# A mixer whose planner, output projection, softmax sums and score products are changed

## The reference

```python
def sandwich(x, y_fn, g_pre, g_post, shift, scale, gate, weight):
    h = rms_norm(x, g_pre) * (1.0 + scale[:, None, :]) + shift[:, None, :]
    y = rms_norm(y_fn(h), g_post)
    return x + weight * gate[:, None, :] * y

# the mixer, one input projection into six parts
qa, ka, va, qb, kb, vb = split(h @ w_in + b_in)
# A: 8 query heads of 64, 2 key heads; own chunk of 64 tokens + 2 before; ALiBi bias, a sink per head
# B: 8 heads of 64; own chunk + 8 before; clipped relative-position bias
p = softmax(q @ k.T / 8 + bias)          # A: exp(sink) is added to the sum
y = concat([rms_norm(oa, g_grp_a), rms_norm(ob, g_grp_b)]) @ w_out + b_out

swiglu = (silu(h @ w_gate) * (h @ w_up)) @ w_down     # inner width 2816
```

## Time and profile before

| | us |
|---|---|
| median of three runs | 1387.67 (1387.14 to 1389.07) |
| profiled execution, its own time | 1383.58 |
| span of its slowest core, which the page shows | 1382.0 |
| spans of the eight cores | 1373.8 to 1382.0 |
| mixer of the first half, L695 to the last chunk | about 301 to 558 |
| mixer of the second half | about 949 to 1215 |

### The profile page before, as it was taken

The page is one execution under the profiler, slowest core; times in us unless marked ns, Lnnn a source line. Parts: engine busy times, 40 slices in busy tenths (PEclk is TensorE's granted clock), DMA queues, the critical chain, the costliest instruction groups (busy, mean ns, idle before and its releaser), DMA issues.

```text
span 1382.0 us, 21264 instructions; the slowest of 8 cores (1373.8 to 1382.0 us)
## 1 busy us (share of the span) xinstructions
PE 1290.0 (93%) x7661; PEld 630.5 (46%) x7661; DVE 468.7 (34%) x866; ACT 442.1 (32%) x870; POOL 191.5 (14%) x382
## 2 busy tenths in 40 slices
PE   2799999999889999999999999999988899999997
PEld 1344444554444544444444444444544454444443
DVE  2131112442543455212442111243245344521122
ACT  2241112333545542111432111233455645311110
POOL 3011001130111112001230001112011011200000
PEclk9999999999999999999999999999999999999999
DMA  9998978657134428994558656202512242899111
GB/s 179 182 191 149 171 126 130 113 86 133 17 69 103 82 51 147 171 154 135 156 151 166 118 110 105 49 1 58 96 32 36 57 70 54 155 166 169 44 47 61
DMA packets 32094, 148.21 MB, mean 107 GB/s; under 512 B 3274, under 2 KB 8567, under 8 KB 20344
## 3 DMA queue, kind: packets, MB, share of 16 engines
q0 software_dynamic: 26128, 129.64, 53.4%
q1 hardware_dynamic: 5864, 17.22, 3.5%
HBM read 258.36 MB, written 8.40 MB: 193 GB/s over the span
## 4 chain that ended last, share of the span: by engine, by line
PE 84%; DMA 5%; DVE 4%; issue 3%; ACT 2%; POOL 1%; DVEq 0%; ACTq 0%; POOLq 0%; another core or an unknown queue 0%
PE psall L660 21%; PE psall L619 17%; PE psall L622 16%; PE psall L774 9%; PE psall L695 6%; PE psall L984 4%; DMA RING<-w_gu 3%; PE psall L882 2%; PE psall L877 1%; PE psall L912 1%; PE psall L650 1%; PE psall L709 1%; DMA R<-w_ada 1%; PE psall L525 1%; DMA RING<-w_in 1%
## 5 line engine op out<-in xcount | busy, mean ns | idle before, releaser
L660 PE MATMUL psall<-R 128*128 128x512 bf16 x1320 | 288.6, 379 | 0.0
L619 PE MATMUL psall<-HT,RING 128*128 128x512 bf16 x928 | 220.9, 381 | 5.4 <-DMA RING<-w_gu 5.3
L629 DVE TENSOR_TENSOR R<-SG,psall 128x512 bf16<-128x512 f32 x136 | 93.5, 688 | 379.2 <-ACT SG L627 353.1
L622 PE MATMUL psall<-HT,RING 128*128 128x512 bf16 x928 | 219.4, 379 | 0.0
L627 ACT ACTIVATE SG<-psall 128x512 f32<-128x512 f32 x136 | 81.2, 597 | 375.1 <-PE psall L622 375.0
L660 PEld LDWEIGHTS psall<-R 128*128 128x128 bf16 x1320 | 128.3, 98 | 151.2
L774 PE MATMUL psall<-HT,RING 128*128 128x512 bf16 x640 | 147.3, 382 | 3.5 <-ACT HT L510 1.7
L619 PEld LDWEIGHTS psall<-HT,RING 128*128 128x128 bf16 x928 | 90.6, 98 | 114.6 <-issue 7.6
L622 PEld LDWEIGHTS psall<-HT,RING 128*128 128x128 bf16 x928 | 90.9, 98 | 109.9 <-issue 0.8
L569 DVE TENSOR_TENSOR XH<-psall,GG 128x1024 f32<-128x1024 f32 x48 | 58.7, 1223 | 205.2 <-ACT SG L561 183.5
L561 ACT ACTIVATE SG<-psall 128x1024 bf16<-128x1024 f32 x48 | 49.1, 1023 | 237.3 <-PE psall L660 188.5
(11 more groups left out here) (136 smaller groups left out, 1109.0 us busy)
## 6 DMA issues: line engine op xcount, KB each, us to landing
RING<-w_gu POOLq DMA_DIRECT2D x53, 1024.0 KB, 10.3
R<-w_down POOLq DMA_DIRECT2D x44, 512.0 KB, 16.9
R<-w_ada POOLq DMA_DIRECT2D x10, 1024.0 KB, 20.3
RING<-w_in POOLq DMA_DIRECT2D x10, 1024.0 KB, 9.7
RING<-w_ada POOLq DMA_DIRECT2D x8, 1024.0 KB, 9.6
out<-X SPq DMA_DIRECT2D x16, 512.0 KB, 2.6
R<-w_gu POOLq DMA_DIRECT2D x5, 1024.0 KB, 53.1
X<-x POOLq DMA_DIRECT2D x8, 512.0 KB, 26.4
```

The source lines that it names most:

```text
L619: e.matmul(PS[bG][:], lhsT=rb[:, k, jj * 128:(jj + 1) * 128], rhs=HT[:, k, tb * 512:(tb + 1) * 512], start=(k == 0), stop=(k == 7))
L622: ins = e.matmul(PS[bU][:], lhsT=rb[:, k, 256 + jj * 128:256 + (jj + 1) * 128], rhs=HT[:, k, tb * 512:(tb + 1) * 512], start=(k == 0), sto ...
L629: S.op('dve', (lambda e, bU=bU, sgi=sgi, j=j, tb=tb: e.tensor_tensor(out=AT[:, tb, j, :], in0=SG[:, sgi, :], in1=PS[bU][:], op=ALU.mult)), ...
L660: ins = e.matmul(PS[bk][:], lhsT=AT[:, t // 4, j, (t % 4) * 128:(t % 4 + 1) * 128], rhs=WD[:, j, hh * 512:(hh + 1) * 512], start=(j == 0), ...
```

## The change

Outside the mixer only names and the model's numbers change. In the mixer:

- **Model.** `LAT` is a number for each engine instead of 0.2 for all; several costs are others, above all that of a value unit.
- **Score products.** `pads`, `QAP` and `QBP` go. `s_pair` does both heads of each partition block together: two table products into two banks, and then products of 64 rows, the lower and the upper half of the partitions in turn, each half into its own bank. For B the heads are put into the order 0, 2, 4, 6, 1, 3, 5, 7.
- **Weight tiles.** Ten `PT` tiles; the four new ones lie where the padded queries were. The mask has a tile of its own.
- **Softmax sums.** For each of the three banks in turn: add the sink's exponential (zero for B), reciprocal, product.
- **Output projection.** The two banks are two steps, each with its own hold, square and gate.

```diff
-EST = {'pe': 0.2, 'act': 0.62, 'dve': 0.68, 'pool': 0.6, 'sp': 0.1}
-LAT = 0.2
+EST = {'pe': 0.2, 'act': 0.55, 'dve': 0.68, 'pool': 0.6, 'sp': 0.1}
+LAT = {'pe': 0.28, 'act': 0.15, 'dve': 0.15, 'pool': 0.15, 'sp': 0.1, 'dma': 0.1}
...
-HORDER = [0, 1, 2, 3, 4, 5, 6, 7]
+HORDER = [0, 2, 4, 6, 1, 3, 5, 7]
...
-    NPT = 6
+    NPT = 10
...
+    def half_square(bank, c):
+        S.op('act', lambda e: e.activation(out=JNK[:, 0:512], in_=PS[bank][:], func=AF.Square, scale=1.0 / 32,
+                                           accum_out=ST[:, c:c + 1]),
+             reads=[ps_key(bank)], writes=[("sg", 0), ("st", c)], cost=0.82)
+
+    def half_gate(t, hh, bank, c):
+        cs = slice(hh * 512, (hh + 1) * 512)
+        S.op('dve', lambda e: e.tensor_tensor(out=XH[:, t % 2, cs], in0=PS[bank][:], in1=GG[:, cs], op=ALU.mult),
+             reads=[ps_key(bank), ("gg",), ("st", c)], writes=[("xh", t % 2)], cost=0.68)
+
+    def half_root(c):
+        S.op('pool', lambda e: e.tensor_tensor(out=ST[:, c:c + 1], in0=ST[:, c:c + 1], in1=ST[:, c + 1:c + 2], op=ALU.add),
+             reads=[("st", c), ("st", c + 1)], writes=[("st", c)], cost=0.35)
...
+            sb_ = [SBANKS[(u + r) % 3] for r in range(2)]
+
+            def fn(e):
+                for r in range(2):
+                    tab = EA[:, ko + 1, r * 4:(r + 1) * 4, :] if kind == "A" else EB[:, tyB[ko], r * 4:(r + 1) * 4, :]
+                    e.matmul(PS[sb_[r]][:], lhsT=IDENTB[:], rhs=tab.rearrange("p h q -> p (h q)"), start=True, stop=False)
+                if kind == "A":
+                    for r in range(2):
+                        rows = slice(r * 64, r * 64 + 64)
+                        ins = e.matmul(PS[sb_[r]][:].rearrange("p (g q) -> p g q", q=128), lhsT=ka[rows, :],
+                                       rhs=QAT[rows, :, tl], start=False, stop=True)
+                else:
+                    for j in range(4):
+                        for r in range(2):
+                            rows = slice(r * 64, r * 64 + 64)
+                            ins = e.matmul(PS[sb_[r]][:, j * 128:(j + 1) * 128], lhsT=kb(j)[rows, :],
+                                           rhs=QBT[rows, j, tl], start=False, stop=(j == 3))
+                return ins
...
-        def tail_b(m):
-            hold[0] = True
-            for hh in range(2):
+        def tail_b(m, hh):
+            hold.add(6 + hh)
...
-                ('pe', lambda: ([("HT", m, 0)], bb), lambda: tail_b(m)),
-                ('act', lambda: (bb, [("sg", 0)]), sq),
-                ('dve', lambda: (bb + [("st", v["q"])], xh), gate),
+                ('pe', lambda: ([("HT", m, 0)], bb[0:1]), lambda: tail_b(m, 0), (6,)),
+                ('pe', lambda: ([("HT", m, 0)], bb[1:2]), lambda: tail_b(m, 1), (7,)),
+                ('act', lambda: (bb[0:1], [("sg", 0)]), lambda: sq(0), ()),
+                ('dve', lambda: (bb[0:1] + [("st", v["c"])], xh), lambda: gate(0), ()),
+                ('act', lambda: (bb[1:2], [("sg", 0)]), lambda: sq(1), ()),
+                ('dve', lambda: (bb[1:2] + [("st", v["c"] + 1)], xh), lambda: gate(1), ()),
...
-            if u < NU and len(pend) < NPT and not blocked:
+            if u < NU and len(pend) <= NPT - 2 and not blocked:
                 def su():
-                    s_unit(u)
-                    pend.append(u)
+                    s_pair(u)
+                    pend.extend((u, u + 1))
```

More of the change, by code:

```diff
@@ L864, in s_unit @@
             ka, kb, va, vb, kk = kv_src(m, ko)
[L865 to L882, removed]
-                                       rhs=QBP[qb_][:, 2 * j:2 * j + 2, :].rearrange("p h q -> p (h q)"),
-                                       start=False, stop=(jj == 1))
-                    return ins
-                rd = kk[1] + [("qbp", qb_), ("eb",), ("identb",)]
@@ L893, in mixer @@
+            S.op('pe', fn, reads=rd + [("ea",), ("eb",), ("identb",)], writes=banks, regions=("R2",), cost=0.85)
+            for r in range(2):
+                pi = (u + r) % NPT
+                S.op('act', (lambda e, r=r, pi=pi: e.activation(out=PT[pi], in_=PS[sb_[r]][:], func=AF.Exp, scale=0.125)),
+                     reads=[banks[r]], writes=[("pt", pi)], regions=(PTR[pi],))
         started = set()
@@ L904, in pv_unit @@
             pi = u % NPT
[L905 removed]
+            slots = [oslot(head(kind, a, i), m) for i in range(4)]
             def fn(e):
@@ L1008, in chain, with sq, gate @@
             bb = [ps_key(6), ps_key(7)]
-            def sq():
-                v["q"], v["p"] = post_square(6, 7)
-            def gate():
-                post_gate(m, 6, 7, v["q"])
-                hold[0] = False
+            ta = lambda: first_free([b for b in (6, 7) if b not in hold])
+            def sq(hh):
+                if hh == 0:
+                    v["c"] = newst(2)
+                half_square(6 + hh, v["c"] + hh)
+                if hh == 1:
+                    v["p"] = None
+            def gate(hh):
+                half_gate(m, hh, 6 + hh, v["c"] + hh)
+                hold.discard(6 + hh)
+                if hh == 1:
+                    v["p"] = half_root(v["c"])
             def fsq():
@@ L1052, in run_due, with free_banks @@
                     run_step(m)
+        def free_banks():
+            return cbanks if late[0] else [b for b in cbanks if b not in hold]
         def source(u):
@@ L1095, in mixer @@
                 save_kv()
-            if not pads4 and not early and u >= first[3]:
-                pads4 = True
-                pads(4)
             if u >= NU and not pend and not late[0]:
@@ L1124, in mixer @@
                 gpos[0] = u
-            if lst and (late[0] or not hold[0]) and ring_state['issued'] > lst[0][0]:
-                t = S.avail('pe', ring_keys(lst[0][0]) + lst[0][1], [ps_key(first_free(cbanks))])
+            if lst and free_banks() and ring_state['issued'] > lst[0][0]:
+                t = S.avail('pe', ring_keys(lst[0][0]) + lst[0][1], [ps_key(first_free(free_banks()))])
                 prio = 3
```

145 lines of the change are left out of this document (63 added, 82 removed).

## The result

The changed kernel took 1370.53 us (median of four runs) against 1387.41 us before on the same chip: ratio 0.9879, 95% interval 0.9863 to 0.9895, so 16.9 us faster. The forecast was 37.5 us. Some runs fall into a slower state at a lower clock; all ratios here leave these out. So the change gives 17 to 23 us, from one measurement to the next. The difference sits in four cores of the first measurement: cores 0 to 3 took 1361.0 us on average in it, as in e9 (1360.8), but cores 4 to 7 took 1364.8 at a granted clock of 0.988, against 1360.7 at 0.993 in e9.

A forecast was written before the change was run, and what follows sets the result against it. TensorE, busy 84% of the chain that ended last, was taken as the bound. Mixer order (-32 us) and row halves (-5.5) summed to -37.5 us, from a median of 1387.67 to 1350 us, range 1327 to 1380.

The forecast's parts named there:

- (a): Mixer order: measured costs, a hold per bank and ten weight tiles cut TensorE's waits; -32 us net.
- the 37 that I had taken: Mixer order's gain before its charge: idle time 26 us, hidden tails 7, clock 4.
- the place without chunks: Second half, last value chunk to first gate chunk: ACT sets the pace, TensorE loses 7 us; net charge 5.
- (b): Score products by row halves: overlap saves 21.7 us, array split switches cost 16.2; -5.5 us.
- R1: Rival in the score pairs: halves overlap and switches are free; -53.7 us, 1334 us, chance 0.27.
- R3: Rival in the score pairs: halves run in turn, each switch waits for the tail; 1390 us, chance 0.05.
- (c): Padding copies on DVE and memsets on POOL that go; 0 us, bounds 0 and -3.
- (d): Added mixer work on ACT, DVE and POOL, such as half squares and gates, beside TensorE; 0, at worst +3 us.
- (e): Late phase and what follows the mixer: order nearly the same, DMA at its limit; 0, at worst +4 us.
- R2: Rival in the attention part: ACT becomes the pace, mixer order gives 12 instead of 32; 1370 us, chance 0.16.

The follow-up runs named there:

- e9: The changed kernel measured again with nothing altered; ratio 0.9836 to the kernel before.
- e11: Changed kernel with ACT's four read-outs of each transposes-back group in the mixer given to DVE; ratio 0.9928 to the kernel before.
- e13: Changed kernel with single score units on padded queries, old unit and head order and six weight tiles; ratio 0.9785 to the kernel before, about 1357 us.
- e5: Kernel before with only the model's numbers replaced by all those of the change; ratio 0.9898 to the kernel before.
- e15: Kernel before with one model number altered, a value unit's cost 0.14 instead of 0.44; ratio 0.9832 to the kernel before.
- e6: Changed kernel with the model's cost of a value unit back at 0.44 instead of 0.14; ratio 0.9965 to the kernel before.
- e2: Changed kernel with both output projection banks as one step again, one hold, square and gate; ratio 0.9881 to the kernel before.
- e8: Changed kernel with six weight tiles instead of ten; ratio 0.9844 to the kernel before.
- e1: Changed kernel with score products on all 128 rows from zero-padded queries, six weight tiles; ratio 0.9839 to the kernel before.
- e10: Changed kernel with each table product directly before its own half of the scores, so halves cannot overlap; ratio 1.0155 to the kernel before, 1408.8 us.
- e4: Changed kernel with second-half chunks paced to last until the first gate chunk; ratio 0.9780 to the kernel before, 1358.7 us.

## Why the prediction was wrong

The direction was right and the time lies in the range; the forecast of 37.5 us was more than twice the 16.9 measured. The two mixer stretches shortened by 17.3 us in sum, which is under the 20 that the prediction had named as a sign of being wrong.

- **The step that failed is (a), -32 us, in its second half.** The first half gave 15 us (13.0 as the mean of eight cores), not far from half of the 37 that I had taken. The second should have given 13.5 after the charge for the place without chunks, and gave 2.3 (4.0 as the mean of eight cores). I had named that place (16 pairs, no chunk), but priced it by ACT's work, 34.8 us against 28 of TensorE, 7 lost. ACT was busy 30.73 of 46 us there, and in e11 less work for it left the place at 45.3 us. What bounds is the wait in turn of a pair on three banks, 1.89 us a pair, against 1.12 for two single units (e13, and e5 without chunks). The price I missed stood in the kernel: `s_deps` takes two of `SBANKS`, which are three. The 12.8 us idle and 3 us of clock of this one place are as much as the whole second half should have gained.
- **What gives the gain.** I credited it to hold, tiles and costs together, and called the order of units the cause. One number, the model's cost of a value unit, gives as much in the kernel before as the whole change (e15), and its old value costs the changed kernel 12 to 18 us (e6). The hold adds some 6 us in the first half (e2), the ten tiles nothing (e8). Pairs are 6 us better than single units in the first half and 17 worse in the second (e9 against e13). Why this number: units of 0.13 us counted 0.44 set the model's TensorE 0.3 us late at each of 202 units. That this made it place units before their exponentials were done is argued from the order, and not tried by itself.
- **(b), -5.5 us,** was right in mechanism, with overlap and two drains in each pair. The size was off: a change takes 0.10 us and not 0.08, and 0.215 - 2 x 0.105 is about nothing, where I had 5.5 us. The length of a pair, 0.85 us, could not tell the forecast from halves in turn (0.86); the starts inside the pair could. R1's free changes and R3's halves in turn are both refuted by the timeline.
- **(c), (d), (e)** held within their bounds: the late phase has no wait on weights, the DVE copies back in e1 cost nothing, and ACT's busy time grew by 5.6 us. Outside the two mixers the kernel takes 2 us more (863.6 to 865.6, mean of eight cores).
- **R2** had the right time, 1370, by the wrong engine: the loss lay in the attention part, but ACT was not the pace.
- The idle time of TensorE was to fall to 13 us; it fell to 28 (9.3 and 18.9 us in the stretches above), which was the sign named for (a) failing.

## What to carry to other kernels

Where a planner orders the work, check its cost of each operation against the trace before adding machinery: one wrong number, put right in the kernel before, was worth as much here as the whole change. Before pairing units, count the buffers: here two of three banks made TensorE and ACT take turns wherever no other work stood between, and both looked idle. A saving by running row halves together must be set against two changes of the array's split. Whether other half-row work put between the changes would pay, no run here tried.

## What the runs showed of the hardware

- Two matmuls of 64 rows in different halves of the array, into different banks, run together: two of 512 columns in the time of one (0.39 us drawn). I had no row for this.
- A change between full rows and row halves costs 0.10 us each way, seen four times in a pair in e10 and twice in the changed kernel.
- In the one place with many short idle gaps (12.8 of 46 us idle) the granted clock fell to 0.93 on the slowest core, where 3 of the 16 us lost were the clock's. It is not a rule: on the eight cores it was 0.81 to 1.00 there, and 1.00 on three. In e4, with 14.8 us idle spread over the whole mixer, it was 1.00 on all eight.
